# Loaded and streamed weight tiles swap their places in the slots of the weight buffers

## What is computed

```python
def swiglu(x, w_gate, w_up, w_down):
    return (jax.nn.silu(x @ w_gate) * (x @ w_up)) @ w_down
```

## Time and profile before

| | |
|---|---|
| runs | 3285.26, 3295.79, 3297.68 us; median 3295.79 us |
| the profiled execution | 3285.75 us, of which span 3283.9 us |
| mean granted clock of TensorE | 0.94 |
| PE busy | 2854.2 us (87%), 17520 matmuls |
| weight loads (PEld) | 2248.3 us (68%) |
| DVE | 2441.1 us (74%) |
| ACT, POOL | 771.0 us (23%), 618.8 us (19%) |
| HBM | 855.89 MB read, 264 GB/s over the span |

### The profile page before, as it was taken

One profiled execution on the slowest core, in us unless ns is written; L12 is line 12 of the kernel. 1 busy time (PEld: TensorE's weight loads), 2 busy tenths in 40 slices (PEclk: granted clock), 3 DMA queues, 4 the chain that ended last, 5 costly groups with the idle time before them and its releaser, 6 DMA issues. The chain is left out here.

```text
span 3283.9 us, 44518 instructions
## 1 busy us (share of the span) xinstructions
PE 2854.2 (87%) x17520; PEld 2248.3 (68%) x17520; DVE 2441.1 (74%) x4651; ACT 771.0 (23%) x1993; POOL 618.8 (19%) x520
## 2 busy tenths in 40 slices
PE   8999987777777889877777777999998999998899
PEld 8889853333333789533333325999887999997898
DVE  7455687777776886877777767878747878877786
ACT  4322222222222343222222222011323001023300
POOL 0000034444444100344444441000000000000000
PEclk9999998888998999988888888999999999999899
DMA  6454699999999637899999996665204666652464
GB/s 211 147 172 155 212 377 419 416 410 419 408 402 421 230 104 237 341 419 417 419 415 399 407 421 253 195 202 162 68 28 154 192 204 185 207 184 87 135 195 148
DMA packets 471089, 868.24 MB, mean 264 GB/s; under 512 B 18912, under 2 KB 399712, under 8 KB 403168
## 3 DMA queue, kind: packets, MB, share of 16 engines
q0 software_dynamic: 73728, 536.90, 39.6%
q1 hardware_dynamic: 396864, 328.24, 31.6%
q10 hardware_dynamic: 288, 0.24, 0.0%
HBM read 855.89 MB, written 9.44 MB: 264 GB/s over the span
## 5 line engine op out<-in xcount | busy, mean ns | idle before, releaser
L2834 PE MATMUL banks<-arena,arena 128*128 128x512 f32 x1744 | 911.6, 681 | 315.7 <-ACT arena L2911 315.7
L2834 PEld LDWEIGHTS banks<-arena,arena 128*128 128x128 f32 x1744 | 370.4, 219 | 838.5 <-issue 448.9
L2792 POOL DMA_INDIRECT arena<-in_peer_uv,arena x512 | 613.8, 1199 | 1310.9 <-PE banks L2834 636.5
L3069 DVE CUSTOM_DVE_ANT_0 arena<-arena,normed 128x1024 f32<-128x1024 f32 x512 | 625.8, 1223 | 226.8 <-DMA arena<-in_peer_uv,arena 224.2
L457 DVE TENSOR_TENSOR weight_ring_part<-weight_ring,weight_high_parts 128x2048 fp32r<-128x2048 f32 (+3 forms) x243 | 537.6, 2212 | 8.3
L3623 PE MATMUL banks<-normed_columns_part,weight_high_parts 128*128 128x256 f32 x1408 | 394.1, 280 | 2.9 <-DVE weight_ring_part L457 2.4
L3624 PE MATMUL banks<-normed_part,weight_high_parts 128*128 128x256 f32 x1408 | 391.8, 278 | 0.0
L3625 PE MATMUL banks<-normed_columns_part,weight_ring_part 128*128 128x256 f32 x1408 | 391.6, 278 | 0.0
L454 DVE CAST weight_high_parts<-weight_ring 128x2048 fp32r<-128x2048 f32 (+3 forms) x243 | 288.6, 1188 | 92.6 <-PE banks L930 64.9
L928 PE MATMUL banks<-weight_high_parts,arena_part 128*128 128x256 f32 x1200 | 337.3, 281 | 7.0 <-PEq L397 3.9
L929 PE MATMUL banks<-weight_ring_part,arena_part 128*128 128x256 f32 x1200 | 334.1, 278 | 0.0
(11 more groups left out here) (606 smaller groups left out, 4265.9 us busy)
## 6 DMA issues: line engine op xcount, KB each, us to landing
weight_ring<-in_ffn_w_gate SPq DMA_DIRECT2D x88, 512.0 KB, 3.7
weight_ring<-in_ffn_w_up SPq DMA_DIRECT2D x88, 512.0 KB, 4.9
weight_ring<-in_ev_w_in SPq DMA_DIRECT2D x33, 1024.0 KB, 5.5
weight_ring<-in_ffn_w_down SPq DMA_DIRECT2D x32, 1024.0 KB, 5.2
weight_ring<-in_od_w_in SPq DMA_DIRECT2D x23, 1024.0 KB, 5.3
weight_ring<-in_peer_wq SPq DMA_DIRECT2D x16, 1024.0 KB, 5.6
weight_ring<-in_xa_wkv SPq DMA_DIRECT2D x13, 1024.0 KB, 5.7
weight_ring<-in_ev_w_out SPq DMA_DIRECT2D x12, 1024.0 KB, 5.4
```

The source lines that it names most:

```text
L2792: pool.indirect_dma_start(out=ring[:, slot(i, s), :], out_offset=None, in_=table, in_offset=bass.IndirectOffsetOnAxis(ap=index[:, i % 2, s ...
L2834: mm = pe.matmul(k.ps[:, 2 * b + half, :], diag[:, g % 2, s, :], v, start=n == b * PEER_TOPK, stop=n == last_mixed[b])
L3069: dve.tensor_tensor_reduce(out=ring[:, here, 0:D], in0=ring[:, here, 0:D], in1=k.xn[:, i % NB, :], scale=1.0, scalar=0.0, op0=ALU.mult, op ...
```

## The change

One line of `tile`: the tiles in `streamed` take the place that all others had, and the others the place of the streamed ones. Loads, splits and products read and write the tiles through `tile` and so move with it; their number, order and waits stay.

```diff
     def tile(self, buffer, slot, n):
         kc, width = self.plan[n][0].shape[1], sum(src.shape[2] for src in self.plan[n])
-        at = LINE * ((slot + (0 if n in self.streamed else 1)) % 2)
+        at = LINE * ((slot + (1 if n in self.streamed else 0)) % 2)
         return buffer[:, slot, at:at + kc * width].rearrange("p (c n) -> p c n", c=kc)
```

## The result

The changed kernel takes 3315.45 us (3309.81 to 3322.96) against 3295.74 us (3285.26 to 3297.68): a ratio of 1.0073, 95% interval 1.0057 to 1.0089, 19.7 us more. It is slower. (The ratios here are those on record; the quotient of the two medians, 1.0060 in this case, differs from them by up to 0.0016.) The profiled execution of after takes 3315.26 us with a span of 3313.4, at its median; that of before was 3285.75 us, some 10 us under its own median. The two spans therefore differ by more, 29.5 us, than the medians do.

What follows compares the result with a forecast made beforehand. Gathers bound two stretches and PE the rest. All terms were 0, so the likeliest case, no change (chance 0.40), kept 3291 us, the mean of the four known times; range 3258 to 3335 us.

Steps and rivals of the forecast that it cites:

- What bounds the kernel: Whole kernel: DMA sets the time in the two expert-gather stretches, PE everywhere else, with a share of 0.945.
- The two levels and their shares: Split products of 256 columns: paces of 113.4 and 117.6 ns, about 40% of the matmuls at the slow one.
- DVE, DMA and plain products at 0: Weight-tile splits, 1 MB tile loads and the fp32 products of line 620: the moved places cost 0 us.
- The split products at 0: Split products of 256 columns: swapping the operands' relative start from 64 bytes behind to 64 ahead was taken as 0 us.
- The price of the rival: Split products: new gap makes the slow pace the rule, costing 26 us if it holds everywhere, 3317 us; chance 0.23.
- All fast become slow: Split products: bound in which 6650 matmuls each lose 4.2 ns, costing 26.4 us after the factor 0.945.
- the two rivals that move the levels: Split products: new gap frees the pair, 3265 us, chance 0.28; or makes the slow pace the rule, 3317 us, 0.23.
- No row shows a third level: Split products: a still slower pace for all, 8.4 ns above the fast one, 3361 us; seen in no row; chance 0.07.
- The picture of the stream that meets the load: Split products: the streamed operand catches up on the weight load; where they meet costs time, 26 us either way.
- The slower rival: Split products: meeting falls near the load's end, delaying each matmul; 26 us more, 3317 us; chance 0.23.
- The formula's 62 us: Split products: N / 2.4 + 2.5 ns gives 109.2 ns for 256 columns, 62 us back, 3229 us; chance 0.02.
- The rule of the undisturbed ports: TensorE's SBUF ports wait for nobody, so the swap is worth exactly nothing at any gap; did not raise the no-change chance.

## Why the prediction was wrong, point by point

**What bounds the kernel: right.** The time outside the gathers is PE's, and a ns on a split product is worth the 11088 x 0.945 that the sum used; outside the gathers the table bears the factor out to within 6.1 us.

**The two levels and their shares: right.** Starts in before give 113.33 and 117.78 ns where the windows gave 113.4 and 117.6, and 39% (loaded) and 44% (streamed) at the slow one where rounded group means gave 40%.

**DVE, DMA and plain products at 0: right**, by the rows of after above.

**The split products at 0: the step that failed.** In place of 0 the new gap costs 2.2 ns on each of them (115.07 to 117.31 and 115.32 to 117.47), 23.1 us by the sum, against 22.3 us outside the gathers and 19.7 by the medians. The 0 rested on two rows. One was that a restart visibly changes the level at an unchanged gap. That is so, but it doesn't follow that the gap has no part: the gap sets how often a run of matmuls takes the fast level, about 6 in 10 at 64 (from 48% to 77% by kind and run) and 1 in 10 at 192 (3 in 10 in one kind of one run). A level also changes without a restart, where gate and up pass into `land`: before, slow until 2844.69 us and fast within half a us behind it, with no pause between these two:

```profile
2844.57 0.28 PE L3625 MATMUL banks<-normed_columns_part,weight_ring_part 128*128 128x256 f32 x1
2844.69 0.29 PE L928 MATMUL banks<-weight_high_parts,arena_part 128*128 128x256 f32 x1
```

So even the observation was narrower than I put it. The other was that the 200-column chunks show no difference between the gaps. They show none in any kernel: 46 paces average 111.8 ns in before, 111.6 in after, 111.7 with the gaps 128 and 0 and with 0 and 128. They keep the pace of the load alone, 112 ns, and so hide whatever the gap does to the stream; it was the nearest row and the wrong witness. My reading is that only in a stream about as long as the load do the two get in each other's way; no stream length between 200 and 256 columns was run.

**The price of the rival: right.** "All fast become slow" was worth 26.4 us and 3317 us; it came to 19.7 (18.8 to 29.3 by the interval) and 3315.45, since a tenth stayed fast. The range, 3258 to 3335, holds the time. This rival had a chance of 0.23. A change that moves nothing but this gap, on a path where the pair already loses 1.4 to 5.6 ns to each other, can act only through it, so the two rivals that move the levels deserved more against the forecast; which of the two, no row of before could tell, since all of them have the gap that turned out the best of twelve.

**"No row shows a third level": true of before, and no bound.** Gap 0 is such a level, 120.0 ns, though not the 8.4 ns above the fast one that I priced at 3361 us but 6.7; it was simply not in the trace of before.

**The picture of the stream that meets the load: fell.** It favours late meetings, so a larger lag of the stream, and 192 over 64. The order found is 64 (115), 224 (117), 192 (117.4), 32 and 96 (118.3), 128 (118.7), 0 and 160 (120): not ordered by any such lag. The slower rival used the same picture with the other sign, so its price came true without its mechanism.

**The formula's 62 us: fell.** The Trainium skill's page "TensorE: Matmul & The Clock Gate", section "Back-to-back issue gap", gave an estimate of 109.2 ns by a formula that the page calls the isolated gap of a single matmul; no mean pace of any gap is under 113.3 ns for 256 columns.

**The rule of the undisturbed ports.** The Trainium skill, page "SBUF — State Buffer", section "SBUF: two separate sides", says PE's ports never wait on anyone, of contention within the engines' side. What the prediction read from it, that the swap is worth nothing at any gap, the trace contradicts: with the same instructions, and DVE, DMA and PE's clock alike, the pace goes from 115 to 120 ns by the places of PE's own two operands. Whether a port waits or something else in PE does, no run here shows.

**Open.** Why a run of matmuls at gap 64 falls into one or the other level, and what in the chip makes 256 bytes the period that orders the table. (A period of 128 is excluded by 64 against 192. By the buffers' sizes the gap 128 is 128 modulo 512 in one of its two kernels and 384 in the other, at one pace, so 512 doesn't fit either.) The 7 us in the gather stretches are open too. The two kernels whose queries all have the gap 64, before and the one with the streamed tiles moved alone, have the shortest sums of these stretches, 1434.3 and 1435.6 us, the other ten 1440.6 to 1448.4; with one trace of each this doesn't tell an effect of the query products from the spread between executions.

## What to carry to other kernels

Where PE is busy without a gap, count the matmuls in a window and compare the pace with that of the load alone; two paces for one and the same line were the sign here that the places of its operands were at stake, and a change of places may then cost time, though it moves no instruction. When a long stream runs against a load of equal length, try the few relative starts of loaded and streamed operand on the chip, and remember that adding a small buffer ahead of them shifts them too (one of 1760 bytes cost 30 us here). Before resting a zero on the nearest row, ask whether that row is bound by something that would hide the effect.

## What the runs showed of the hardware

Matmuls of 256 columns in the fast fp32 format, each with its own load of 128 columns, run at the full granted clock at a few mean paces, by the start of the loaded operand relative to the streamed one modulo 256 bytes: 113.33 and 117.78 ns at 64 and 192, 120.0 at 0, about 118.7 at 128. At gap 0 and gap 128 the pace is the same whichever operand is the weight tile; at 48 and 80 it isn't, by 0.4 to 0.9 ns. The two levels at 64 and 192 can each be held over hundreds of matmuls: in after one run of 1449, from 2041 to 2212 us, is at 117.78 throughout. Weight tiles eight bytes off the best place cost as much as the worst gap did (41.9 against 42.6 us). Streams of 200 columns keep 111.6 to 111.8 ns at all gaps, and the plain fp32 products of line 620 between `gain_row` and the weight ring 379 to 380 ns.
